# A two-layer transformer kernel: the norms between its sub-blocks, and the matmuls on either side of them, in two ranges of 256 tokens

## The reference

```python
def pre(x_in, i):
    return rms_norm(x_in, norm_pre[l, i]) * (1.0 + mod[:, i, 1]) + mod[:, i, 0]
def post_add(x_in, y, i, res_w):
    return x_in + res_w * mod[:, i, 2] * rms_norm(y, norm_post[l, i])
x = post_add(x, swiglu(pre(x, 0), ffn_w_in[l, 0], ffn_w_out[l, 0]), 0, FFN_RES)
y = token_mixer(pre(x, 1), ...)
x = post_add(x, y, 1, 1.0)
x = post_add(x, swiglu(pre(x, 2), ffn_w_in[l, 1], ffn_w_out[l, 1]), 2, FFN_RES)
```

## Time and profile before

| | |
|---|---|
| median of three runs | 3354.19 us (3351.44 to 3356.36) |
| the profiled execution: time, span | 3349.84 us, 3348.0 us |
| busy share of the span: TensorE, VectorE, GpSimd, ScalarE | 96%, 62%, 40%, 35% |
| mean granted TensorE clock, as a share of 2.4 GHz | 0.975 |
| first block of two layers | up to about 1022 us |
| exits of layer 0 of the second block (TensorE restarts) | 1421.5, 1816.4, 2191.9 us |
| exits of layer 1 | 2570.7, 2966.6, the last one from 3328 us on |

### The profile page before, as it was taken

How to read it: one execution, slowest core, us unless ns; L and a number is a source line. 1 busy time by engine, 2 the same in 40 slices (tenths; PEclk the granted TensorE clock), 3 DMA queues, 4 the chain that set the end, 5 groups by cost and what they waited for, 6 DMA issues and landing times.

```text
span 3348.0 us, 43790 instructions
## 1 busy us (share of the span) xinstructions
PE 3199.6 (96%) x16130; PEld 2534.0 (76%) x16130; DVE 2070.9 (62%) x2722; ACT 1162.9 (35%) x1798; POOL 1337.2 (40%) x569
## 2 busy tenths in 40 slices
PE   8999999999996999899998999999998999989998
PEld 6757787757775888787677888878887876878887
DVE  3777785777785445898377443464459964774422
ACT  3355323355323223333434222422233335332233
POOL 3402343402333445544153445634464531534454
PEclk9999999999997999999999999999998999999999
DMA  4524472624553332667142332333235871423332
GB/s 128 186 82 126 145 226 74 190 74 130 151 176 93 98 94 82 97 112 102 55 122 64 114 94 84 103 88 100 85 92 82 129 103 33 142 76 100 92 86 73
DMA packets 577892, 358.73 MB, mean 107 GB/s; under 512 B 50946, under 2 KB 528588, under 8 KB 577484
## 3 DMA queue, kind: packets, MB, share of 16 engines
q1 hardware_dynamic: 573908, 350.23, 40.7%
q10 hardware_dynamic: 3832, 6.42, 0.5%
HBM read 343.75 MB, written 10.49 MB: 106 GB/s over the span
## 4 chain that ended last, share of the span: by engine, by line
PE 57%; DVE 7%; DMA 2%; SPq 1%; POOL 1%; ACT 1%; issue 1%; ACTq 0%; POOLq 0%; DVEq 0%
PE bank L166 18%; PE bank L168 17%; PE bank L167 17%; DMA w_raw<-in_mix_w_in_dram 2%; SPq L1754 1%; POOL w_lo L160 1%; DVE xT L2493 1%; DVE w_s L2378 1%; PE bank L2059 1%; PE bank L2038 1%; PE bank L2071 0%; PE bank L2018 0%; DVE y_s L2481 0%; DVE th_s L2500 0%; PE bank L2034 0%
## 5 line engine op out<-in xcount | busy, mean ns | idle before, releaser
L160 POOL TENSOR_TENSOR w_lo<-w_raw,w_hi 128x1024 fp32r<-128x1024 f32 (+1 forms) x556 | 1329.2, 2396 | 1975.2 <-ACT w_hi L150 1972.4
L166 PE MATMUL bank<-xh,w_lo 128*128 128x512 f32 x2432 | 973.8, 400 | 47.2 <-DVE xl L2458 28.1
L167 PE MATMUL bank<-xl,w_hi 128*128 128x512 f32 x2432 | 955.7, 393 | 0.0
L168 PE MATMUL bank<-xh,w_hi 128*128 128x512 f32 x2432 | 955.6, 393 | 0.0
L150 ACT ACTIVATE w_hi<-w_raw 128x1024 fp32r<-128x1024 f32 (+1 forms) x556 | 566.1, 1021 | 781.6 <-PE bank L168 673.4
L166 PEld LDWEIGHTS bank<-xh,w_lo 128*128 128x128 f32 x2432 | 462.4, 190 | 162.2 <-issue 47.5
L167 PEld LDWEIGHTS bank<-xl,w_hi 128*128 128x128 f32 x2432 | 463.0, 190 | 98.4 <-issue 4.8
L168 PEld LDWEIGHTS bank<-xh,w_hi 128*128 128x128 f32 x2432 | 461.8, 190 | 98.5
L166 PE MATMUL bank<-HH_s,w_lo 128*128 128x512 f32 x704 | 274.2, 389 | 0.0
L168 PE MATMUL bank<-HH_s,w_hi 128*128 128x512 f32 x704 | 273.9, 389 | 0.0
L167 PE MATMUL bank<-HL_s,w_hi 128*128 128x512 f32 x704 | 273.9, 389 | 0.0
(11 more groups left out here) (509 smaller groups left out, 4276.1 us busy)
## 6 DMA issues: line engine op xcount, KB each, us to landing
w_raw<-in_ffn_w_in_dram SPq DMA_DIRECT2D x176, 512.0 KB, 3.8
m_raw_l<-in_mod_w_dram SPq DMA_DIRECT2D x128, 512.0 KB, 5.0
w_raw<-in_w_in_dram SPq DMA_DIRECT2D x78, 512.0 KB, 4.0
w_raw<-in_mix_w_in_dram SPq DMA_DIRECT2D x64, 512.0 KB, 9.7
w_raw<-in_ffn_w_out_dram SPq DMA_DIRECT2D x64, 384.0 KB, 3.4
w_raw<-in_ffn_w_out_dram SPq DMA_DIRECT2D x64, 320.0 KB, 3.2
m_half_l<-in_mod_w_dram SPq DMA_DIRECT2D x32, 256.0 KB, 2.8
w_raw<-in_w_out_dram SPq DMA_DIRECT2D x16, 512.0 KB, 4.7
```

Source lines behind the costliest of these rows:

```text
L160: ins = nc.gpsimd.tensor_tensor(to(ring.lo[s]), of(ring.raw[s]), to(ring.hi[s]).bitcast(F32), ALU.subtract)
L166: nc.tensor.matmul(out, wl, xh, start=start, stop=False)
L167: nc.tensor.matmul(out, wh, xl, start=False, stop=False)
L168: return nc.tensor.matmul(out, wh, xh, start=False, stop=stop)
```

## The change

An exit is done for two ranges of tokens, `tok[0]` = 0 to 255 and `tok[1]` = 256 to 511 (in the packed statistics, `rows_of`: partitions 0 to 63 and 64 to 127). The last output tile is computed by matmuls of 256 columns, each range in its own PSUM bank. In a feed-forward the order over (column, range) is (0,0) (0,1) (1,0) (1,1) (2,0) (3,0) (2,1) (3,1): both ranges behind each other for the first two weight columns, range by range for the last two. In the mixer's last tile range 0 comes wholly before range 1. The sums, roots and spreads exist once for each range: those of range 0 are issued in and behind the last tile, those of range 1 from inside the next `products`, after 8, 16 and 24 of its steps. `products` runs over all blocks and tiles for range 0 and then for range 1, so each of its weight tiles is loaded twice as often, for matmuls of 256 columns; a block comes free in range 1 only. VectorE's four operations per tile become eight of half the width; ScalarE's queue holds the weight splits of the last tile in another order (`exit_tail`). `low` and `shift` take a range as well, as does the entry norm (`pre00`, `pre01`); the six banks of sums and spreads become `sums`, `tail`, and two each for `post` and `pre`. The last exit of all does `part` in halves and the addition whole.

```diff
-    for label, b in (("sq0", 7), ("ysq0", 6), ("ycr0", 5), ("post0", 4), ("pre1", 7)):
+    for label, b in (("sums0", 7), ("tail0", 6), ("post00", 4), ("pre10", 5), ("post01", 6), ("pre11", 7)):
...
-        def products(labels, n0, x, x_lo, at, banks=None):
+        def products(labels, n0, x, x_lo, at, banks=None, tail=None):
 
             banks = banks or [free(pe, label) for label in labels]
-            order = [(k, b) for k in range(KT - 2) for b in range(4)] + [(k, b) for b in range(4) for k in (KT - 2, KT - 1)]
-            for k, b in order:
-                if b == 0:
-                    pe.wait_ge(s["h_split"], at + k + 1)
-                wh, wl = weights(n0 + b, b) if k == 0 else (ring.hi[b], ring.lo[b])
-                cc = slice(k * P, k * P + P)
-                last = mm3(nc, banks[b], wh[:, cc], wl[:, cc], x[:, k, :], x_lo[:, k, :], k == 0, k == KT - 1)
-                if k == KT - 1:
-                    last.then_inc(ring.used, 1)
+            for hf in range(2):
+                if hf == 0:
+                    order = sorted(((k, b) for k in range(KT) for b in range(4)), key=lambda kb: (kb[0] + (0, 0, 1, 2)[kb[1]], kb[1]))
+                else:
+                    order = [(k, b) for k in range(KT - 2) for b in range(4)] + [(k, b) for b in range(4) for k in (KT - 2, KT - 1)]
+                split = 0
+                for i, (k, b) in enumerate(order):
+                    if k + 1 > split:
+                        split = k + 1
+                        pe.wait_ge(s["h_split"], at + 8 * hf + split)
+                    wh, wl = weights(n0 + b, b) if k == hf == 0 else (ring.hi[b], ring.lo[b])
+                    cc = slice(k * P, k * P + P)
+                    last = mm3(nc, banks[b][:, tok[hf]], wh[:, cc], wl[:, cc], x[:, k, tok[hf]], x_lo[:, k, tok[hf]], k == 0, k == KT - 1)
+                    if hf and k == KT - 1:
+                        last.then_inc(ring.used, 1)
+                    if tail is not None and hf == 0 and i in (7, 15, 23):
+                        tail((i - 7) // 8)
...
+        def spread_half(hf, label, r):
+
+            out = free(pe, f"{label}{hf}")
+            h = rows_of[hf]
+            for g in (2 * hf, 2 * hf + 1):
+                one_row = ident[h, 32 * g:32 * g + 1].broadcast_to([P // 2, P])
+                last = nc.tensor.matmul(out[:, g * P:(g + 1) * P], one_row, r[h, :], start=True, stop=True)
...
+        def tail_sums(i, hf):
+
+            out = free(pe, f"sums{i}") if hf == 0 else held(f"sums{i}")
+            groups = (2 * hf, 2 * hf + 1)
+            kinds = [("sq", sqt), ("ysq", ysq), ("ycr", ycr)] if i < EXITS else [("sq", sqt)]
...
+            def part(j, x, start, stop):
+                for g in groups:
+                    last = nc.tensor.matmul(out[32 * g:32 * g + 32, j * P:(j + 1) * P], ones[:, 2, 0:32],
+                                            x[:, g * P:(g + 1) * P], start=start, stop=stop)
+                return last
+
+            for j, (kind, x) in enumerate(kinds):
+                part(j, tot[kind], j == 0, False)
+            for j, (kind, x) in reversed(list(enumerate(kinds))):
+                if kind == "ysq":
+                    pe.wait_ge(s["y_square"], 9 * i + 8 + hf)
+                elif kind == "ycr":
+                    pe.wait_ge(s["y_cross"], 9 * i + 8 + hf)
+                elif hf == 0:
+                    pe.wait_ge(*taken(i, TAIL))
                 else:
-                    pe.wait_ge(s["y_square" if label == "ysq" else "y_cross"], 8 * i + KT)
-                last = sums(held(f"{label}{i}"), x[(KT - 1) % 2], False, True)
+                    wait_read(pe, f"tail{i}")
+                last = part(j, x[TAIL % 2] if kind != "sq" else sqt[TAIL % 2], False, j == 0)
...
+        def second_half(i):
+
+            def run(step):
+                if step == 0:
+                    tail_sums(i, 1)
+                elif step == 1:
+                    spread_tail(i, 1, f"post{i}", post_r, 3 if i < EXITS else 2)
+                elif i < EXITS:
+                    spread_tail(i, 1, f"pre{i + 1}", pre_r, 4)
+
...
+            i = 2 * sub
+            pe.wait_ge(evac[TAIL % 2], TAIL // 2 + turn[f"out{sub}"][TAIL % 2])
+            outs = [bank[TAIL % 2], free(pe, f"tail{i}")]
+            for b, hf in ((0, 0), (0, 1), (1, 0), (1, 1), (2, 0), (3, 0), (2, 1), (3, 1)):
+                wh, wl = weights(4 * TAIL + B_OF[sub] + b, b)
+                for k in range(CUT[b], CUT[b + 1]):
+                    cc = slice((k - CUT[b]) * P, (k - CUT[b] + 1) * P)
+                    last = mm3(nc, outs[hf][:, tok[hf]], wh[:, cc], wl[:, cc], HH[:, k, tok[hf]], HL[:, k, tok[hf]], k == 0, k == FT - 1)
+                    if hf and (b, k - CUT[b]) == (2, 4):
+                        first_half(i, 0)
+                if hf:
+                    last.then_inc(ring.used, 1)
+                elif b == 3:
+                    last.then_inc(s["tail"], 1)
+            first_half(i, 1)
+            first_half(i, 2)
+            if i == EXITS:
+                second_half(i)(0)
+                second_half(i)(1)
+            elif i == 2:
+                own.tail = second_half(2)
...
+        wh, wl = weights(B_MO + TAIL, TAIL % 4)
+        for hf in range(2):
+            out = free(pe, "tail1" if hf else ("mo", TAIL))
+            for k in range(KT):
+                cc = slice(k * P, (k + 1) * P)
+                last = mm3(nc, out[:, tok[hf]], wh[:, cc], wl[:, cc], MH[:, k, tok[hf]], ML[:, k, tok[hf]], k == 0, k == KT - 1)
+                if hf and k == 4:
+                    first_half(1, 0)
+            last.then_inc(ring.used if hf else s["tail"], 1)
+        first_half(1, 1)
+        first_half(1, 2)
...
+        def exit_tail(i, src, splits, last, done):
+
+            for n in splits[0:2]:
+                hi(n)
+            take_half(i, 0, src)
+            post_root(i, 0)
+            if i < EXITS:
+                pre_root(i, 0)
+            for n in splits[2:3]:
+                hi(n)
+            act.wait_ge(ring.used, done)
+            take_half(i, 1, src)
+            if i == EXITS:
+                post_root(i, 1)
+                hi(last)
+                return
+            shift(i + 1, 0, 0)
+            hi(last)
+            shift(i + 1, 0, 1)
+            shift(i + 1, 0, 2)
+            post_root(i, 1)
+            shift(i + 1, 0, 3)
+            shift(i + 1, 0, 4)
+            pre_root(i, 1)
+            for k in range(5, KT):
+                shift(i + 1, 0, k)
             for k in range(KT):
-                shift(i, k)
+                shift(i + 1, 1, k)
...
+                def whole(k):
+                    for hf in range(2):
+                        c = tok[hf]
+                        ins = V.tensor_tensor(y[:, k, c], y[:, k, c], held(f"{label}{hf}")[:, c], MUL)
+                        if k == KT - 1:
+                            read(ins, f"{label}{hf}")
+                        else:
+                            step.mark(ins)
+                    at[k] = step.n
...
+            pre_root(i, 0)
+            dve.wait_ge(s["root_spread"], 1 - E0 + root_count(i, 1))
+            part(0, 0)
+            added(0, 0)
+            dve.wait_ge(s["root_spread"], 1 - E0 + root_count(i, 2))
+            scaled(0, 0)
+            cross_half(i, 1)
+            order = [(hf, k) for hf in range(2) for k in range(KT)]
+            for n, item in enumerate(order):
+                if n + 1 < len(order):
+                    if n + 1 == KT:
+                        dve.wait_ge(s["root_spread"], 1 - E0 + root_count(i, 4))
+                    part(*order[n + 1])
+                    added(*order[n + 1])
+                    scaled(*order[n + 1])
+                low(i + 1, *item)
+                if item == (0, 2):
+                    post_root(i, 1)
+                if item == (0, 4):
+                    pre_root(i, 1)
+            dve.wait_ge(to["h_split"], 16 * to_i + 2 * KT)
```

More of the change, by code:

```diff
@@ L1853, in sums @@
             return last
-        def spread_root(n, label, r):
-            out = free(pe, label)
-            pe.wait_ge(s["root_ready"], n)
-            for g in range(TT):
-                one_row = ident[:, 32 * g:32 * g + 1].broadcast_to([P, P])
-                last = nc.tensor.matmul(out[:, g * P:(g + 1) * P], one_row, r, start=True, stop=True)
+        def spread_half(hf, label, r):
[4 more added lines that the diff above has]
+                last = nc.tensor.matmul(out[:, g * P:(g + 1) * P], one_row, r[h, :], start=True, stop=True)
             last.then_inc(s["root_spread"], 1)
@@ new lines, in post_root, with pre_root @@
+        def post_root(i, hf):
+            h = rows_of[hf]
+            act.wait_ge(s["mean_ready"], mean_count(i, hf))
+            ins = nc.scalar.activation(post_r[h, :], held(f"sums{i}")[h, 0:P], ACT.Sqrt, bias=eps[h, 0:1])
+            if i == EXITS and hf:
+                read(ins, f"sums{i}")
+            else:
+                ins.then_inc(s["post_std"], 1)
+        def pre_root(i, hf):
```

(44 more changed lines are left out.)

243 lines of the change are left out of this document (126 added, 117 removed).

## The result

The changed kernel is slower: 3423.97 us, median of four runs (3422.36 to 3428.85), beside 3353.29 us for the kernel before, measured with it; ratio 1.0212, 95% interval 1.0195 to 1.023. The forecast was 3425. Its profiled execution took 3424.64 us, with a span of 3422.9 and a mean granted clock of 0.972. Between the two spans lie 74.9 us, between the two medians 70.7: the profiled execution of the kernel before was 3.4 us shorter than this median.

The account below looks back on a forecast made before the run. TensorE was busy 96% of the span, but VectorE was taken to pace the stretch behind exits. 12.3 + 25.0 + 29.8 + 3.0 + 1.0 = +71 us on 3349.84 gives 3421, with 4.35 for the median 3425; range 3378 to 3448.

Parts of the forecast that it names:

- The price of halves (a tile in halves 3.4, matmul 0.121): VectorE's four operations take 1.70 us per half tile, 3.4 per tile instead of 2.77; a 256-column matmul takes 0.121 us.
- VectorE is thus already the slightly slower of two engines.: Behind the restart, before the change: VectorE takes 2.77 us per tile, TensorE's twelve matmuls 2.72, for eight tiles.
- S: TensorE's restart after an exit; at exit 2 of layer 0 forecast 1.5 us earlier than before.
- The sums (0.7 us): Range 0's 24 small matmuls, now inside the last tile's stream, add 0.7 us; range 1's again cost 0.7 in the group.
- R: Start of VectorE's first reciprocal at an exit; at exit 2 of layer 0 forecast 2.5 us earlier than before.
- E: Time origin at exit 2 of layer 0: the end of the last main matmul's slot before the change, 2178.18.
- The stalls: VectorE behind the restart at exit 2 waits 3.2 us for range 1's roots, then 2.1 for its second spread.
- rival 1: Slower but with few stalls: each of five exits 7.4 us less, +34, 3388; chance 0.22.
- The second chain (2.5 + 0.95 us): Range 1's work on VectorE behind the restart: reciprocal and five small operations 2.5 us, then a second reciprocal.
- Exit 0: First exit of both layers: tot_sq, held to 1406.66, stalls the stream; +15.0 us in layer 0, +14.8 in layer 1.
- Here VectorE's own lateness counts.: At exit 0, VectorE's last operation moves from 1437.9 to 1452.9, delaying SyncE's wait for Kn and further weights: +15.0.
- Rivals 2, 3 and 4: TensorE stays slower, 3340 (0.05); half matmuls' weight load not hidden, 3540 (0.08); VectorE's extra work hides, about -2 (0.03).

Follow-up runs that it names:

- order_only: The kernel before with only the order in ranges, in half width; last output tile, sums, roots and spreads stay whole and single: 3370.48 us, ratio 1.0054.
- half_vector: The kernel before with VectorE's four operations per tile at five exits each issued as two of 256 columns: 3362.31 us, ratio 1.0026.
- sums_first: The changed kernel with range 1's sums before the matmul group, its spreads after steps 11 and 19, its first root one shift earlier: 3396.58 us.
- order_chain: order_only with the second chain's seven small operations added on VectorE, on scratch and waited for by nobody else: 3391.39 us, ratio 1.0111.
- sums_after_tail: The changed kernel with range 0's sums behind the whole last output tile instead of inside it: 3430.6 us, ratio 1.0226.

## Why the prediction was right, step by step

The forecast and its mechanism held: VectorE paces the stretch, and the halves, the second chain and its stalls make the time. That it came within 1 us of the median is in part luck, though. In the profiles the change costs 74.9 us where the sum has 71, and in that sum terms that were too small stand against one that was never paid.

**The price of halves (a tile in halves 3.4, matmul 0.121).** Right where it counts. Halves with a wait between them keep 1.70 us per half tile (order_only, the changed kernel), and half matmuls have a pitch of 0.120.

**"VectorE is thus already the slightly slower of two engines."** Wrong for the kernel before. Paces of 2.77 and 2.72 us say little while TensorE starts at half clock: kept awake it finished the group 1.5 us sooner with the same VectorE. For the sum it mattered little, since the lengths behind S were set against the measured 24.1. But the same words made me expect +27 from half_vector, where the slack left 9; and the +4.7 per exit that my sum gave order_only was +3.4.

**The sums (0.7 us).** Too small by half, twice per exit. The prediction took 8 small matmuls at 0.23 us from the earlier trace rows; there the eight sum all four groups of 128 tokens. With two groups there are four, and they take as long: 2228.20 to 2228.44 in the trace above, 1.4 us for the 24. Why half as many take as long no run here shows. In the last tile this makes its growth 2.5 us and not 1.7 (the stream ends 340.1 us after the block of the exit before, where it was 337.6). So R, forecast at E+0.4, came at E+1.1, 338.7 us after that block.

**R and S.** S = R+9.5 instead of R+11.85: the first `xl` slipped in ahead of GpSimd and the next add was held instead, the alternative that the text names; the end of the group doesn't move by it. From R to the next block: forecast 49.75, measured 50.8. With R 0.7 late that is the 1.8 by which exit 2 exceeds the forecast.

**The stalls.** Forecast 3.2 and 2.1, measured 4.1 and 2.5 at exit 2, and 5.2 and 3.1 at exit 1, where the granted clock of the whole stretch was 0.78. At exit 2 0.7 of the first one's excess of 0.9 is again the sums; the clock adds to it. I let TensorE be "partly cold" in the three steps ahead of the sums; behind its gaps it worked at 1.2 GHz for longer (at exit 2 the 18 half matmuls from 2224.36 to the sums took 3.8 us, where the pitch of 0.12 gives 2.2), at exit 1 in the stretch after each stall:

```profile
1834.60:1839.60 5.00, 5.00 (x39) 4.36 (x38) 0.00 (x0) 0.28 (x1) 0.00 (x0) 0.60 0.06 16
1839.60:1844.60 5.00, 0.71 (x4) 0.51 (x4) 4.58 (x12) 1.47 (x4) 0.00 (x0) 0.75 0.00 0
1844.60:1849.60 5.00, 5.00 (x26) 4.66 (x25) 4.76 (x11) 1.04 (x3) 0.00 (x0) 0.57 0.00 0
```

(windows as above: while VectorE stands still in the first, TensorE works at 0.60, and again at 0.57 behind its own gap.) The stalls are thus 1.3 us longer at exit 2 and 3.0 at exit 1, where R to the next block is 51.3 us instead of 47.65. sums_first shows the stalls to be worth 27 us; it is the kernel nearest to rival 1 (few stalls), 3397 where I had 3388.

**The second chain (2.5 + 0.95 us).** Right: order_chain pays 3.8 per exit. With order_only's 17, the chain's 21 and the stalls' 27, 65 of 70.7 us are shown by runs. The rest is argued: the tails, GpSimd's second hold and two spreads, less the earlier root (6.6 from sums_after_tail).

**Exit 0.** The way to R was right. All of layer 0's feed-forward comes 3.9 us later (2.3 + 1.6, as above). With these taken off, `tot_sq` ended at 1406.7, where 1406.66 was forecast, and TensorE stood 2.6 us inside its tail, where the forecast gives some 2.4. Then it went on at half clock for a while:

```profile
1410.76 0.41 PE L1903 MATMUL bank<-tot_sq_s,ones 128*32 128x128 f32 x4 [2.60 <-DVE tot_sq_s L2568]
...
1412.36 0.58 PE L166 MATMUL bank<-HH_s,w_lo 128*128 128x256 f32 x1
1412.74 0.41 PE L167 MATMUL bank<-HL_s,w_hi 128*128 128x256 f32 x1
```

R came 0.75 us later than forecast, again by the sums, and R to S was 2.35 shorter, as at exit 2. This exit alone puts the next block 14.1 us later, where some 12 was forecast.

**"Here VectorE's own lateness counts."** This is the term that was not paid, some 3 us at each exit 0. SyncE's wait for `Kn` did grow, from 16.7 us in its list of waits before (two times, one per layer) to 25.2. Yet from the block behind exit 0 to the last output tile TensorE's mixers took 1.7 and 2.3 us less than before: a new wait for `Btr_s` (4 us per layer) stands against shorter ones for `PT_s` and `th_s` (14.5 us in all before, 1.4 after). The wait for `Kn` itself was not tried alone. The size was misread, too. The `xl` at 2207.51 in the earlier trace rows is that of the last tile but one; in a wider view the line covers both and ends at 2209.13:

```profile
2207.51 1.62 DVE L2458 SCALAR_TENSOR_TENSOR xl<-th_s,modc,xh 128x512 fp32r<-128x512 f32 x2
```

VectorE's last operation at exit 0 so ended at 1438.8 and not at 1437.9, and the +15.0 should have been +14.1; with the same in layer 1 the sum would be 69 and not 71. The 2.7 of layer 1 has no row either; the shift of R for exit 0 above it is 2.5.

**The balance.** Against the forecast by rows the entry cost 0.9 us more, the five exits about 8 in all, the end 0.5, and the lateness through `Kn`, some 6, was not paid: 71 and 4 are 75.

**Rivals 2, 3 and 4** are excluded: TensorE waited for `xl` all along, the half matmul cost 0.12, and the time moved by 2%.

## What to carry to other kernels

A join that is split in two costs its serial part twice: the second range brings its own sums, root and spread, and they land on the engine that already paces the restart. Before one counts on an earlier restart, ask which engine will pace the stretch behind it, and place the second range's sums where the first still leaves TensorE idle. Two engines with equal paces are not equally tight, if one of them starts at half clock: filler work ahead of the restart was worth 1.0 to 1.5 us each time and 6 to 7 us in all, more than either way of moving GpSimd's hold.

## What was not expected of the hardware

Sixteen float32 matmuls of identity by identity in a gap of 4.7 us had the granted clock at 1.00 from the restart on, at all five exits; over the gap itself it was 0.89 at exit 2. Four small matmuls for the sums of two groups of tokens took as long as eight for four groups, 0.22 to 0.24 us. Two half operations of VectorE with no wait between them take 0.75 to 0.88 us a pair (3.16 us for a tile's eight), those with waits between them 3.40 for the same eight. Pairs also differ from those in being halves of one tile; which of the two matters wasn't tried. And a hold of 1.73 us by GpSimd was worth under 1 us, because a spread of 2.05 us ran beneath it.
